# A two-layer hybrid block: the decay exponents of layer 2's mixers made by TensorE products, a tile ahead, and read out of PSUM by the exponential

## The reference

```python
def lower_exp_diff(cs):
    n = cs.shape[-1]
    tril = jnp.tril(jnp.ones((n, n), dtype=bool))
    diff = cs[..., :, None] - cs[..., None, :]
    return jnp.where(tril, jnp.exp(jnp.where(tril, diff, 0.0)), 0.0)
...
    a_cs = jnp.cumsum(da, axis=-1)
    lmat = lower_exp_diff(a_cs)
    scores = jnp.einsum('bclhn,bcshn->bhcls', cc, bc) * lmat
...
    gc = jnp.cumsum(g.reshape(bsz, nc, CHUNK, GDN_HEADS).transpose(0, 3, 1, 2), axis=-1)
    decay = lower_exp_diff(gc)
    strict = jnp.tril(jnp.einsum('bhcid,bhcjd->bhcij', kbeta, kc) * decay, -1)
    qk = jnp.einsum('bhcid,bhcjd->bhcij', qc, kc) * decay
```

## Time and profile before

| | us |
|---|---|
| runs | 2251.28, 2251.50, 2252.94 |
| median | 2251.5 |
| profiled execution, span from its first to its last instruction | 2258.5 |
| TensorE busy in the span | 2216.4 (98%), 13052 products |
| VectorE busy | 1581.9 (70%) |
| ScalarE busy | 914.2 (40%) |
| GpSimd busy | 263.5 (12%) |
| mean granted TensorE clock | 0.990 of full |

### The profile page before, as it was taken

One profiled execution on the slowest core, in us unless ns is written; L12 is line 12 of the kernel. 1 busy time (PEld: TensorE's weight loads), 2 busy tenths in 40 slices (PEclk: granted clock), 3 DMA queues, 4 the chain that ended last, 5 costly groups with the idle time before them and its releaser, 6 DMA issues. The chain is left out here.

```text
span 2258.5 us, 34288 instructions
## 1 busy us (share of the span) xinstructions
PE 2216.4 (98%) x13052; PEld 1823.0 (81%) x13052; DVE 1581.9 (70%) x2212; ACT 914.2 (40%) x1672; POOL 263.5 (12%) x266
## 2 busy tenths in 40 slices
PE   8999999999999999999999989999999999999997
PEld 7888888888888887887877777887888888888886
DVE  5657678876665545657687788887798777765557
ACT  5443544343343321243344445555533333324444
POOL 0222232100000000001232222322020000000000
PEclk9999999999999999999999989999999999999999
DMA  4111111144333264433233442323235444448655
GB/s 152 47 38 58 37 56 38 66 147 157 116 114 111 86 261 175 150 111 122 85 112 112 150 141 72 107 93 112 96 131 191 163 158 163 158 156 299 214 181 184
DMA packets 106952, 289.06 MB, mean 128 GB/s; under 512 B 9692, under 2 KB 35388, under 8 KB 102332
## 3 DMA queue, kind: packets, MB, share of 16 engines
q1 hardware_dynamic: 106812, 287.14, 36.2%
HBM read 205.01 MB, written 82.10 MB: 127 GB/s over the span
## 5 line engine op out<-in xcount | busy, mean ns | idle before, releaser
L124 PE MATMUL psG<-h_hi,w_hi 128*128 128x512 f32 (+1 forms) x624 | 164.4, 395 | 2.1 <-DVE features_T L1875 1.6
L124 PE MATMUL psG<-h_hi,w_lo 128*128 128x512 f32 (+1 forms) x624 | 161.6, 391 | 0.0
L124 PE MATMUL psG<-h_lo,w_hi 128*128 128x512 f32 (+1 forms) x624 | 161.4, 392 | 0.0
L455 POOL TENSOR_TENSOR sb_w<-sb_left 128x128 f32<-128x128 f32 (+3 forms) x96 | 96.9, 1014 | 320.3 <-DVE sb_left L582 320.3
L124 PEld LDWEIGHTS psG<-h_hi,w_hi 128*128 128x128 f32 x624 | 109.9, 188 | 23.7 <-DVE features_T L1875 2.9
L124 PEld LDWEIGHTS psG<-h_hi,w_lo 128*128 128x128 f32 x624 | 111.4, 188 | 20.2 <-DVE w_lo L155 0.2
L124 PEld LDWEIGHTS psG<-h_lo,w_hi 128*128 128x128 f32 x624 | 111.1, 188 | 20.1 <-issue 0.5
L582 DVE TENSOR_TENSOR_SCAN sb_left<-sb_left 128x128 f32<-128x128 f32 (+3 forms) x96 | 102.7, 1078 | 2.1 <-ACT sb_left L468 1.4
L150 ACT CAST w_hi<-w_raw 128x1024 fp32r<-128x1024 f32 x48 | 50.3, 1049 | 120.0 <-PE psG L124 61.7
L155 DVE TENSOR_TENSOR w_lo<-w_raw,w_hi 128x1024 fp32r<-128x1024 f32 x48 | 58.6, 1222 | 55.0 <-ACT w_hi L150 55.0
L2024 POOL TENSOR_TENSOR features_T<-m_bias_both 128x512 f32<-128x512 f32 x10 | 16.8, 1675 | 680.3 <-DMA m_bias_both<-in_proj_pairs 633.0
(11 more groups left out here) (657 smaller groups left out, 5949.8 us busy)
## 6 DMA issues: line engine op xcount, KB each, us to landing
w_raw<-in_units SPq DMA_DIRECT2D x76, 512.0 KB, 4.3
w_raw<-hidden_blocks SPq DMA_DIRECT2D x77, 256.0 KB, 2.9
merge_gates<-features_T SPq DMA_DIRECT2D x12, 1024.0 KB, 6.7
merge_gates<-merge_gates SPq DMA_DIRECT2D x12, 1024.0 KB, 4.8
features<-features_T SPq DMA_DIRECT2D x24, 512.0 KB, 3.8
w_spare<-in_units SPq DMA_DIRECT2D x22, 512.0 KB, 4.4
down_sums<-w_spare SPq DMA_DIRECT2D x22, 512.0 KB, 3.3
hidden_blocks<-features_T SPq DMA_DIRECT2D x11, 1024.0 KB, 3.9
```

Source lines behind the costliest of these rows:

```text
L124: return pe.matmul(out, lhs, rhs, start=first, stop=last, skip_group_check=True)
L455: pool.tensor_tensor(w, left_chunk(S, 1), left_chunk(S), ALU.subtract).then_inc(w_ready, 1)
```

## The change

The exponent of head h at (row s, column t) is made as a sum of products in one PSUM bank: mask + (sum of column t) - (sum of row s). A group has 3 heads x 128 = 384 columns, so 12 heads are 4 groups. For each group TensorE makes a pair of products in fp32r into bank 2 (`decay_exponents`): the identity times the mask, repeated for three heads, and a product over 32 partitions (of which 8 are filled) of `decays_own` with `decays_rows`. Those hold, for each group, the negated sums in a high and a low part, and constants -1 and 1 at the places that pick a head. ScalarE rounds both to fp32r (`decays_rounded`, two casts) and later takes each group's exponential out of PSUM (`decayed`, 384 columns). VectorE's subtraction and minimum are gone.

All of this happens a tile ahead: tile n's round makes the exponents and exponentials of tile n + 1 behind `yo`, `wt`/attention, the first half of `y`, and `stn`. Tile 0's are made ahead of all tiles (`first_decays` and the last lines of ScalarE's list). `tr2` of a tile waits for the last exponential `L3`. In the projections, ScalarE's multiplication and VectorE's subtraction out of PSUM take the place of VectorE's copy; SyncE writes 24 rows in two copies, puts constants by 12 small copies, and loads a tile's sums with 8 small copies (6 x 128, and 2 x 3 x 128 values); GpSimd fills the two buffers once. Three constant matrices that nobody reads are no longer loaded.

```diff
+def load_decays(sp, D2, acs_rows, n):
+    tok = slice(n * P, (n + 1) * P)
+    for g in range(DECAY_GROUPS):
+        pieces = acs_rows[2 * DECAY_HEADS * g:2 * DECAY_HEADS * (g + 1), tok]
+        sp.dma_start(D2.decays_own[32 * g:32 * g + 2 * DECAY_HEADS, :], pieces).then_inc(D2.decays_here, 16)
+        sp.dma_start(D2.decays_rows[32 * g + 2 * DECAY_HEADS:32 * g + 2 * DECAY_HEADS + 2, :, :],
+                     pieces.rearrange("(h q) t -> q h t", q=2)).then_inc(D2.decays_here, 16)
...
 # layer2_projections, SyncE
                 if m == DECAY_PAIR + 2:
                     sp.wait_ge(small_read, 4)
-                    sp.dma_start(acs_rows.rearrange("t (h p) -> h t p", h=NH),
-                                 small_T[0:NH, :].rearrange("h (t p) -> h t p", t=NT)).then_inc(D2.rows_kept, 16)
+                    for q, piece in enumerate((decays_hi, decays_lo)):
+                        sp.dma_start(acs_rows.rearrange("(h q) t -> q h t", q=2)[q], piece).then_inc(D2.rows_kept, 16)
+                    sp.wait_ge(D2.decays_zeroed, 2)
+                    for g in range(DECAY_GROUPS):
+                        for r in range(DECAY_HEADS):
+                            at = 32 * g + 2 * r
+                            sp.dma_start(D2.decays_rows[at:at + 2, r, :], C["one"][at:at + 2, :]).then_inc(D2.decays_here, 16)
+                if m == DECAY_PAIR + 3:
+                    sp.wait_ge(D2.rows_kept, 32)
+                    sp.wait_ge(D2.decays_here, DECAYS_ONCE)
+                    load_decays(sp, D2, acs_rows, 0)
...
 # layer2_mixers, SyncE
-            sp.wait_ge(D2.rows_kept, 16)
             sp.dma_start(BIAS, bias_in[0].rearrange("p (a b) k -> p a (b k)", a=2)).then_inc(bias_here, 16)
-            decays(0)
...
             weights(0, 4)
+            scalL.wait(sp, "rows", 0)
+            load_decays(sp, D2, acs_rows, 1)
...
-                vectF.wait(sp, "sd1", n - 1)
-                decays(n)
+                if n < LAST:
+                    scalL.wait(sp, "rows", n)
+                    load_decays(sp, D2, acs_rows, n + 1)
...
 # ScalarE
+            def decays_rounded(n):
+                a.wait_ge(D2.decays_here, DECAYS_ONCE + DECAYS_EACH * (n + 1))
+                tensL.wait_last(a, "d3", n)
+                scalL.done("own", a.copy(D2.decays_r[:, 0, :], D2.decays_own))
+                scalL.done("rows", a.copy(D2.decays_r[:, 1:, :], D2.decays_rows[:]))
+            def decayed(n, g):
+                tensL.wait(a, f"d{g}", n)
+                if n and g == 0:
+                    vectF.wait(a, "sd1", n - 1)
+                scalL.done(f"L{g}", a.activation(DEC[:, DECAY_HEADS * g:DECAY_HEADS * (g + 1)].rearrange("p h t -> p (h t)"),
+                                                 PS[:, 2, 0:DECAY_HEADS * P], ACT.Exp))
...
-                if front and n:
-                    decayed()
+                if later_decays:
+                    decays_rounded(n + 1)
...
 # VectorE
-                if front:
-                    v.wait_ge(dec_here, 16 * n + 16)
-                    vectF.done("dsub", tt(DEC[:], DEC[:], per(PT[:, PACS:PACS + NH], NH, P), ALU.subtract))
-                    vectF.wait(v, "dsub", n)
-                    vectF.done("dmask", v.scalar_tensor_tensor(DEC[:], DEC[:], 0.0, over(MSK[:, 0, :], NH), ALU.min, ALU.add))
...
 # TensorE
+            def decay_exponents(n, g):
+                if g == 0:
+                    scalL.wait(pe, "rows", n)
+                    if n:
+                        scalF.wait(pe, "pt", n - 1)
+                else:
+                    scalL.wait(pe, f"L{g - 1}", n)
+                out, r = PS[:, 2, 0:DECAY_HEADS * P], slice(32 * g, 32 * g + 32)
+                mm(out, ident_r[:], over(mask_r[:], DECAY_HEADS), True, False)
+                tensL.done(f"d{g}", mm(out, D2.decays_r[r, 0, :], D2.decays_r[r, 1:, :].rearrange("p h t -> p (h t)"), False, True))
...
                     turn(tensF, "tr1", 1, [F[:, c] for c in range(GQ0, GQ0 + 4)])
-                    scalF.wait_last(pe, "pt", n)
+                    scalL.wait(pe, "L3", n)
```

More of the change, by code:

```diff
@@ L1615, in layer2_projections @@
         over_tiles = lambda r: r.unsqueeze(1).to_broadcast([P, NT, NH])
-        par_here, ws_hi_done, prepared, small_done, small_read = (sem(n) for n in (
-            "par_here", "ws_hi_done", "prepared", "small_done", "small_read"))
+        par_here, ws_hi_done, prepared, small_done, small_read, rows_hi_done = (sem(n) for n in (
+            "par_here", "ws_hi_done", "prepared", "small_done", "small_read", "rows_hi_done"))
         full, z_done = sem("full"), sem("z_done")
@@ L2262, in layer2_mixers @@
         scalG = Steps(sem("scalar_chain"), "T2 yq0 yq1 yln yexp T4 mtm T8 T16 T32 vu0 vu1 va vo1 vo0 T64 wt vn osq oln oexp")
-        vectF = Steps(sem("vector_front"), "ss ssc nqk kb qg swab mx mx2 ngm sdif dsub dmask nc0 nc1 nc2 nc3 nt qkd sd0 sd1 den rden "
+        vectF = Steps(sem("vector_front"), "ss ssc nqk kb qg swab mx mx2 ngm sdif nc0 nc1 nc2 nc3 nt qkd sd0 sd1 den rden "
                                            "yo yx att st1 y yz st2")
-        scalQ, scalL, tensY = Steps(sem("scalar_queries"), "qt"), Steps(sem("scalar_decays"), "L"), Steps(sem("tensor_off"), "yo")
+        scalQ, tensY = Steps(sem("scalar_queries"), "qt"), Steps(sem("tensor_off"), "yo")
+        tensL, scalL = Steps(sem("tensor_decays"), "d0 d1 d2 d3"), Steps(sem("scalar_decays"), "own rows L0 L1 L2 L3")
         vectX, vectN = Steps(sem("vector_xdt"), "xdt xdec"), Steps(sem("vector_blocks"), "m1 vt1 v0")
@@ L2349, in _ @@
             vectN.wait(sp, "vt1", LAST)
+            tensL.wait(sp, "d3", LAST)
             sp.dma_start(GN, g_pre.to_broadcast([P, D])).then_inc(gn_here, 16)
@@ L2513, in tile @@
                 prod = earlier(t) if t != LAST else None
+                later_decays = front and n < LAST
                 if chain:
@@ L2646, in tile @@
                         squared_sum(prod, X, Y[:])
+                if later_decays:
+                    decayed(n + 1, 0)
+                if chain:
                     tensG.wait(a, "vn", i)
                     scalG.done("vn", a.copy(VN[:], PS[:, 5, 256:512]))
+                if later_decays:
+                    decayed(n + 1, 1)
+                if chain:
                     if front and t is not None:
@@ L2652, in tile @@
                         high(3)
+                if later_decays:
+                    decayed(n + 1, 2)
+                if chain:
                     tensG.wait(a, "o", i)
@@ L2658, in tile @@
                     scalG.done("oexp", a.activation(orr, orr, ACT.Exp, scale=-0.5))
+                if later_decays:
+                    decayed(n + 1, 3)
+                if chain:
                     if front and t is not None:
@@ L2692, in end @@
                 high(7)
+            a.copy(ident_r[:], C["ident"][:]).then_inc(masks_r, 1)
+            a.wait_ge(c_here, 16)
+            a.copy(mask_r[:], MSK[:, 0, :]).then_inc(masks_r, 1)
+            decays_rounded(0)
+            for g in range(DECAY_GROUPS):
+                decayed(0, g)
             tiles(tile)
@@ L2871, in tile @@
                 if front:
-                    scalL.wait(v, "L", n)
+                    scalL.wait(v, "L3", n)
                     tensF.wait(v, "qk", n)
@@ L2996, in _ @@
             tensG.open(pe)
+            tensL.open(pe)
             tensY.open(pe)
@@ L3346, in half_unit, with first_decays @@
                 half_products(pe, W, U0 + b, G[b], h_hi, h_lo, 0, first, last)
+            def first_decays():
+                pe.wait_ge(masks_r, 2)
+                for g in range(DECAY_GROUPS):
+                    decay_exponents(0, g)
             def end():
@@ L4264, in layouts @@
     return {k: np.ascontiguousarray(v) for k, v in L.items()}
-CONSTS = ("ident", "before", "minus_from", "minus_one", "upto", "one")
+CONSTS = ("ident", "upto", "one")
 def build(nc, A, out):
```

58 lines of the change are left out of this document (39 added, 19 removed).

## The result

The changed kernel takes **2279.6 us** (median of four runs, 2277.65 to 2283.5) against 2251.5 us (2251.28 to 2252.94): a ratio of 1.0112, with an interval of 1.0095 to 1.0129. It is slower by 28 us, where my sum gave 17.5 and the forecast 2269.0. The profiled execution took 2279.73 us, with a span of 2277.9 us.

The account below looks back on a forecast made before the run. TensorE was taken to bound steady tiles, VectorE tiles 0 and 1. Five tiles at 2.1 us (+10.5) plus +7 for the start gave +17.5 us on the 2251.5 median: 2269.0 us, own range 2260 to 2279, whole range 2253 to 2281.

Parts of the forecast that it names:

- What bounds the kernel: Layer-2 mixers: TensorE alone bounds tiles 2 to 6, so relieving VectorE there was priced at nothing; VectorE bounds tiles 0, 1.
- The number of tiles that pay: Steady layer-2 tiles: five tiles pay 2.1 us each, +10.5 us; tile 7 pays nothing.
- The full 0.17: Steady tile on TensorE: each of eight 384-column products costs 0.17 us, 1.36 us per tile.
- the sentence on the 32-row product: Each pair's second product: it might cost 0.04 instead of 0.17 us, a tile 0.84; the full price was taken.
- The switches between formats: Two isolated pairs per steady tile between fp32 products: 0.26 us extra each, 0.5 us per tile.
- What the single bank costs: All four groups use bank 2: stalls of 0.1 us at groups 1 and 2, 0.2 us per tile.
- Rival 2: Ping-pong: three whole exponentials exposed per steady tile and ScalarE's tail late, +11.5 us, 2280.5 us; chance 0.12.
- The start: Rounds ahead of tile 0 (+5 us), then tiles 0 and 1: together +7 us (0 to +11) by tile 1's end.
- in tile 0 VectorE gives back 3.5 us: Tile 0: VectorE's removed operations return 3.5 us, so its decay-weighted blocks start at about +1; tile 1 likewise.
- Rival 1: The half-speed clock stretch from 1335 to 1355 us goes, worth 8 us: 2261 us, still slower; chance 0.15.
- Rival 3: The pairs fill true gaps in TensorE's steady tile; only the start is left, +3: 2254.5 us; chance 0.10.
- Rival 4: Faster: steady-tile gaps and waits shrink as VectorE is relieved, five tiles gain 11.5 us: 2243 us; chance 0.11.

Follow-up runs that it names:

- e4: Kernel before without VectorE's subtraction and minimum of each decay, nothing put in their place: 2253.29 us, ratio 0.9987.
- e3: Changed kernel without the second product of each pair, so the exponents are the mask alone: 2266.77 us, ratio 1.0049.
- e8: Kernel before without VectorE's subtraction and minimum, and with tile 0's exponential moved ahead on ScalarE, behind the copy of QT: 2249.87 us, ratio 0.9986.
- e2: Changed kernel with each pair's second product summing over all 128 partitions instead of 32 (decays not the reference's): 2268.36 us, ratio 1.0060.
- e10: Changed kernel with the 32-row product of each pair issued twice in a row (decays not the reference's): 2288.79 us, ratio 1.0148.
- e1: Kernel before, unchanged, profiled and timed a second time: 2253.87 us, ratio 0.9999.
- e9: Changed kernel, unchanged, profiled and timed a second time: 2278.81 us, ratio 1.0106 to the kernel before.
- e6: Changed kernel with tile 0's own four pairs moved from ahead of everything into tile 0, alternating between banks 5 and 6: 2275.94 us, ratio 1.0104.
- e7: Changed kernel with each pair's second product summing over 64 partitions instead of 32 (decays not the reference's): 2281.00 us, ratio 1.0122.
- e11: Changed kernel with tile 0's pairs moved inside tile 0 and the output-weight casts ahead of tile 1's exponentials: 2276.39 us, ratio 1.0115.
- e5: Changed kernel with ScalarE's four casts of output weights in tile 0 moved ahead of tile 1's four decay exponentials: 2276.93 us, ratio 1.0107.
- e12: Changed kernel with tile 0's pairs inside tile 0, casts ahead of tile 1's exponentials, and second products over 128 partitions: 2260.99 us, ratio 1.0029.

## Why the prediction was right in its sign and short in its size

**What bounds the kernel** held. The chain of a steady tile is TensorE alone before and after, and e4 shows the removal at nothing there: 35.20, 35.18, 35.19 and 35.19 us. VectorE's share is 24.26 of 35, 69%, where I had some 70%.

**The number of tiles that pay.** I counted five of 2.1 us. Four intervals pay 3.2 us, and one of them (5-6) 0.8 more, which the profile shows as one piece that the weight-load queue stood for nothing named (a like piece stands in the interval 6-7 in e3). I have no cause for that. The interval from tile 2 to tile 3 seems to pay nothing: 35.18 us with the change, 35.01 and 35.02 in e8 and e4. But TensorE pays for the pairs there too. The changed kernel and e2 ran it at full clock:

```profile
1369.56:1404.75 35.19, 33.11 (x482) 25.92 (x475) 24.61 (x60) 17.54 (x53) 9.49 (x14) 1.00 0.13 38
```

```profile
1364.69:1398.33 33.64, 31.55 (x483) 25.99 (x475) 24.54 (x60) 17.53 (x53) 9.49 (x14) 1.00 0.14 42
```

128 rows make it shorter by 1.55 us, the four passages again. What hides the price is the clock of the kernel before: in that interval its mean granted clock was 0.95 and 0.82 in its two profiles (33.53 and 37.96 us) and 0.90 in e4 and e8. Length times clock is 31.1 to 31.9 us in these four, and 35.2 with the change. That is an estimate, since a wait does not scale with the clock, and no profile of the kernel before ran this interval at full clock.

**"The full 0.17"** was right for the product (0.17 to 0.19 in e2 and e10) and wrong for its place. The step that failed is the sentence on the 32-row product: I weighed whether it would be cheaper by its rows, and never what it costs to leave the 128 rows for one product and return. The term was missing: 1.57 us per tile, 6.3 us in the last four intervals. The hint stood in the trace of before: rows over 64 partitions in the earlier trace rows come 0.32 us apart where the first of them follows a product over 128 rows, and only 0.22 apart where they follow their like, as in tile 0 of the kernel before:

```profile
1294.10 0.49 PE L3010 MATMUL m_ps<-m_k_prev,m_aqk 64*128 64x128 f32 x4
1294.42 0.39 PE L3010 MATMUL m_ps<-m_aqk 64*128 64x128 f32 x4
1294.64 0.39 PE L3010 MATMUL m_ps<-m_k_prev,m_aqk 64*128 64x128 f32 x4
1294.87 0.39 PE L3010 MATMUL m_ps<-m_aqk 64*128 64x128 f32 x4
```

The Trainium skill has a rule for it, too, which I did not weigh: "TensorEngine Tiling (Array Packing)", section "Tiling Modes", says under its key properties that a change of the tiling mode drains TensorE, though it gives no figure. It does not say whether a single product over fewer rows is such a change. The runs agree with it if that is so, and give a figure, 0.39 us for a passage and back. The rule that I did cite, that one product over 32 rows takes as long as one over 128, agrees with e10's 0.18 us beside e2's 0.17.

**"The switches between formats"**, 0.5 us per tile, were over-priced: e3's four isolated masks cost 0.90 us together, of which the products are 0.68 to 0.72, so 0.2 is left. **"What the single bank costs"**, 0.2 us, was nothing: no wait for an exponential in a steady tile. Rival 2 falls with it.

**"The start"** was short by half: +7 forecast, 7.4 + 5.4 + 1.2 = 14 us measured between e1 and e9. Its parts: the rounds ahead of tile 0 took 1.88 us each, where I had 1.27. With the mask product alone (e3) a round took 1.26 us, and with 128 rows (e2) 1.58, both at a granted clock of 0.50. So a product cost 0.32 us there, the exponential and the ways there and back 0.94 where I had 0.59, and the passages 0.30. The first transposes began at 1294.6, not 1292 to 1293. The casts of the output weights did come late and TensorE stood 2.9 us for them, where I had 1.5. The first interval of the changed kernel also ran at a granted clock of 0.89 and 0.85 in the two profiles, where the kernel before had full clock (27.98 us), and length times clock, 28.4 us, differs from that by 0.4 only: most of what it lost is the clock. And "in tile 0 VectorE gives back 3.5 us", with the same again for tile 1, failed: e4 shows 0 and 0.7. A share of 33.48 of 35 us is no proof that an engine sets the pace; most of this work stood where VectorE would have waited for ScalarE in any case. In tile 1 the pairs did find room: from e1 to the changed kernel TensorE's busy time in interval 1-2 rose by 3.2 us, from 32.16 to 35.38, and its idle time fell by 2.0, from 2.88 to 0.91, so only 1.2 us are seen.

**The rivals.** Rival 1, the low stretch, can't be judged as I put it: the stretch from 1335 to 1355 was the profiled execution's and no property of the kernel before, so its going was worth nothing against the median, and new low windows came at the start. One tile later something like it is seen: in the interval 2-3 both profiles of the kernel before, e4 and e8 have low windows, and five profiles with all 32- or 64-row pairs (the changed kernel, e9, e6, e7, e11) have none. But e5 and e10, with such pairs, have one again, and of e2, e3 and e12 only e2 has none. Whether the change or chance did that is not shown. Rival 3 is refuted in the steady tiles, by 3.2 us each, and holds in part in tile 1. Rival 4 is refuted by e4 and e8: even at no price at all the relief is worth 0.14%. The lesson in the sum itself: I set +17.5 against both the profiled span and the median, though the span held a stretch that the median did not.

**The sum as measured:** 14 (start, tiles 0 and 1) + 12.8 (four intervals of 3.2) + 0.8 + 0.2 (tile 2, beside e4 and e8 with their low windows) = 27.8 us, beside 28 between the medians. Still open are the 0.8 us of interval 5-6, and what brings the clock down in one execution and not in the next. A version with the right decays and 128 rows, which needs stationary operands that are zero outside their group, wasn't tried; e12 bounds what it could reach.

## What to carry to other kernels

Before work is moved onto the engine that ends last, measure what its removal is worth with nothing put in its place: here such runs say 0.13 and 0.14%, some 3 us, about what the pairs cost in a single tile. An engine busy for 96% of a stretch may still be followed by a wait that swallows whatever it is relieved of; look at what its next consumer waits for, and at the order of the queue that makes it. And price a product with few rows by its neighbours: between 128-row products the round trip (0.39 us) cost twice what the product did (0.18), so such products belong next to their like.

## What the runs showed of the hardware

- Leaving 128 rows for 64 costs TensorE the same as leaving them for 32: steady tiles of 38.38 and 38.36 us.
- A product over 32 rows and 384 columns right behind another costs 0.18 us, the same as one over 128 rows.
- With 128 rows the weight load of the second product starts 0.17 us ahead of its product; with 32 or 64 rows the two start together (e2, changed kernel, e7).
- The granted clock of the same program, the kernel before, fell to 0.50 from 1335 to 1355 in one profile and from 1367 to 1372 in the next. In e5 it stood at 0.50 from 1380 to 1405, and that interval took 15 us more than in the changed kernel (50.16 against 35.18).
